# The opening of a two-block transformer kernel by feature blocks, with products on strips of TensorE's array

## The chip, the cores and the metric

The kernel runs on one core of a Trainium2 chip. Its engines work side by side and meet at semaphores: TensorE (matrix products; PE in the rows, PEld its weight loads), VectorE (DVE), ScalarE (ACT), GpSimd (POOL) and SyncE (SP), which here only issues loads. The metric is the device time of one execution in microseconds, lower is better. Three runs of the kernel before took 1216.97, 1219.66 and 1221.44 us.

## The reference

Two blocks of a network on 256 tokens of 1024 features, in float32. Only the start of the first block matters here:

```
mod(c)   = silu(c) @ w_ada + b_ada            # shift sh1, scale sc1, ...
h        = rmsnorm(x, g_mix) * (1 + sc1) + sh1
h_ctx    = rmsnorm(ctx, g_mix) * (1 + sc1c) + sh1c     # sh1c, sc1c from mod(c_ctx)
z        = h @ w_in  -> q, k, v, g, dd (32 columns), cb, cc, ch, ga, gb
zd       = dd @ w_dec_up + b_dec              # for two directions
log_a    = log_sigmoid(zd) / 16
o        = gated linear attention, forward and backward, over q, k, v, log_a,
           its start states from the same on ctx (k, v, log_a only)
```

Then come a convolution branch, gates, three feed-forward parts and a second block with two attentions.

## The kernel before

**Units.** The weights pass through the core in units of 256 columns (1 MB), loaded by SyncE into a ring of three buffers `raw`. ScalarE rounds a unit to `whi` (a short form of float32), VectorE takes the rest `wlo = raw - whi`, and TensorE makes three products for each: high by high, high by low, low by high. The activations are split in the same way: `A_hi`, `A_lo` for x and `B_hi`, `B_lo` for ctx. The order of the units of block one is the list `P1`: dd, two k, four v, two q, then the rest. The units dd, k and v are made for x and for ctx; a k or v unit has 96 products with a moving side of 256 columns. Every engine walks the same list in a loop over `u`, in which ScalarE first empties the PSUM banks of unit u - 1 (`evac1`), then rounds unit u + 2 (`split`), then does its part of the attention (`gla_front`, `gla_step`). The order on each engine is the order in which the code is written; nothing is reordered.

**The opening.** It must turn the two vectors c and c_ctx into shift and scale columns (one column for each block of 128 features), and x and ctx into the modulated, transposed, split activations. SyncE loads eight tiles `ada0[j]` of the modulation weights (1 MB each; tiles 0 to 3 give the shift, 4 to 7 the scale), the small vectors, ctx and x, then the units. TensorE multiplies the silu of c and c_ctx (two columns on the stationary side) by each tile (`L1272`, 2x256 outputs), turns the resulting row into columns (`L1756`), and transposes the normalized ctx and x (`norm`, `L1340`). ScalarE applies shift and scale to ctx (`modulate(0)`), VectorE to x (`affine`), both round and take rests. All 16 columns of all eight tiles are ready before the first feature is modulated. The dd unit follows with 48 products, then k0.

**The decays.** After the first half of k0 TensorE runs `decay_products` (passes 0 and 1; passes 2 and 3 follow within k1). A pass g is a direction and a pair of heads. ScalarE takes absolute values, exponentials and logarithms (`log_decays`, `soft_part`, `decays`), VectorE minima and running sums (`log_decays`, `sums`). These stand in the queues of both engines ahead of later splits and evacuations.

**GpSimd** computes 16 further modulation rows with its own multiply and add tree (`load_ada`, `adapt`, lines 748 and 756 to 759), one unit after the other, each load behind the end of the unit before. The first load waits for the opening's columns (`as_mm`), the first unit for the last rest of the activations (`hlo_done`, 16).

```
load_ada(0)
pool.wait_ge(hlo_done, 16)
for n in range(8):
    adapt(n)
    load_ada(n + 1)
```

Of the kernel before, what the change touches and what calls it, by code (L numbers as in the profile page):

```python
# [10 lines left out]
ALU = mybir.AluOpType  # L11
# [135 lines left out]
def build(nc, a, out):  # L147
    with ExitStack() as ctx:
# [72 lines left out]
        arow = ada_raw[0:2, :, :].rearrange("p a b -> p (a b)")  # L221

        ddT = arena[0:2 * RANK, 20 * KB:22 * KB].rearrange("p (s t) -> p s t", s=2)
# [21 lines left out]
        wdec = arena[0:2 * RANK, 77 * KB:81 * KB].rearrange("p (d n) -> p d n", d=2)  # L245
# [7 lines left out]

        XN = at3(24, TT, D)
        HF = at3(32, KD, T)
        HF1 = [at3(0, KD, T), at3(8, KD, T)]
# [63 lines left out]
        ada0_mm = sem("ada0_mm")  # L320
        ada0_row = sem("ada0_row")
# [145 lines left out]
        def unit_source(kind, n):  # L467
# [7 lines left out]
            if kind in first:  # L475
                w, c0 = first[kind]
                return cview(w, c0 + UC * n), KD, UC
# [20 lines left out]
        def _(sp):  # L498
            def load_unit(u, kind, n):
# [3 lines left out]
                dst = raw[ring(u)][:, 0:k * w].rearrange("p (k w) -> p k w", k=k)  # L503
# [49 lines left out]
            for j in range(8):  # L553
                if j == 2:

                    for name, r0 in VEC.items():
                        v = a[name]
                        n = math.prod(v.shape) // P
                        src = bass.AP(tensor=v.tensor, offset=0, ap=[[P, n], [1, P]])
                        sp.dma_start(vrows[r0:r0 + n, :], src).then_inc(vec_in, 16)  # L560
                    for name, r0, n in (("b_ada", 0, 48), ("b_ada_2", 48, 72)):
                        src = bass.AP(tensor=a[name].tensor, offset=0, ap=[[P, n], [1, P]])
                        sp.dma_start(brows[r0:r0 + n, :], src).then_inc(vec_in, 16)
                sp.dma_start(ada0[j], a["w_ada"][0].rearrange("(p k) n -> p k n", k=KD)[:, :, UC * j:UC * j + UC])\  # L564
                    .then_inc(start_ada[j], 16)
                if j == 3:
                    sp.dma_start(ctxX, a["ctx"].rearrange(tok, p=P)).then_inc(x_in[0], 16)
                    sp.dma_start(X[:], a["x"].rearrange(tok, p=P)).then_inc(x_in[1], 16)

            for u, (kind, n) in enumerate(P1):  # L570
                load_unit(u, kind, n)
# [37 lines left out]

        def norm_bank(n, b):  # L610

            return {0: (4, 5, 6, 0), 1: (1, 2, 3, 4), 2: (5, 6, 7, 2), 5: (4, 6, 7, 2)}.get(n, (4, 5, 6, 2))[b]
# [20 lines left out]

        def norm_fp32(n):
            return HF1[n] if n < 2 else HF

# [27 lines left out]
        def q_order(g):  # L664

            return 2 * (g % 2) + g // 2 + 1
# [1824 lines left out]
```

## Time and profile before

| | us |
|---|---|
| median of three runs | 1219.66 |
| profiled execution | 1218.4 |
| its span | 1216.6 |
| TensorE busy | 1166.5 (96%) |
| VectorE busy | 853.4 (70%) |
| ScalarE busy | 574.0 (47%) |
| GpSimd busy | 325.1 (27%) |

The busy rows of the page cut the span into 40 equal slices; a digit is the busy share in tenths, and PEclk the granted clock of TensorE in tenths of full speed. Rows of the timeline give the start, the time until the end of the last instruction merged into the row, and in brackets the idle time ahead and what ended it. A row that says x2 counts two instructions.

### The profile page before, as it was taken

The page shows a single profiled execution, that of the slowest core. Times are in us where ns is not written, and L with a number is a line of the kernel's source. Part 1 is how long each engine was busy: PE and PEld are TensorE (multiplying, and loading weights), DVE is VectorE, ACT ScalarE, POOL GpSimd, SP SyncE. Part 2 cuts the span into 40 slices and gives each one's busy share as a digit, 9 for nine tenths or more (in the row PEclk, how much of TensorE's full clock was granted, in tenths as well). Part 3 has the DMA queues.
Part 4 walks back from the last instruction along what each step waited for, and adds up shares of the span by engine and source line. Part 5 has one row for each costly group of instructions (what it writes and reads, how often), then busy time and mean ns, then how long its engine had stood idle before and what let it go on. Part 6 is the DMA issues. An engine that isn't in the chain of part 4 may idle for free.

```text
span 1216.6 us, 18692 instructions
## 1 busy us (share of the span) xinstructions
PE 1166.5 (96%) x7600; PEld 1040.7 (86%) x7600; DVE 853.4 (70%) x935; ACT 574.0 (47%) x734; POOL 325.1 (27%) x219
## 2 busy tenths in 40 slices
PE   6899999999999899999989999999999989999996
PEld 2599988999999888888878888889998989888885
DVE  0478474489577778877778877788766587755676
ACT  1566434354443364444555444445654625544452
POOL 1376573066565200000020000011156663000000
PEclk9899999999999899999989999999999989999999
DMA  9643645365866648777747777755954655656670
GB/s 310 218 139 105 208 144 168 105 217 186 273 232 218 203 169 275 242 254 257 267 147 255 254 252 246 261 161 190 298 181 149 201 186 179 204 177 201 213 258 35
DMA packets 192354, 250.59 MB, mean 206 GB/s; under 512 B 4763, under 2 KB 171870, under 8 KB 192158
## 3 DMA queue, kind: packets, MB, share of 16 engines
q1 hardware_dynamic: 183838, 217.44, 54.9%
q0 software_dynamic: 8448, 32.18, 7.7%
q8 instruction: 50, 0.82, 0.3%
q14 instruction: 18, 0.15, 0.0%
HBM read 248.56 MB, written 1.05 MB: 205 GB/s over the span
## 4 chain that ended last, share of the span: by engine, by line
PE 77%; DVE 13%; ACT 4%; issue 3%; SPq 2%; DMA 1%; POOL 0%; POOLq 0%; DVEq 0%; ACTq 0%
PE twin L1272 74%; DVE arena L1819 4%; DVE wlo L1819 3%; ACT arena L838 2%; DVE arena L1827 2%; SPq L564 1%; DMA raw<-in_w_in 1%; ACT whi L838 1%; PE twin L1340 1%; DVE X L1819 1%; DVE A_both L1819 1%; PE twin L1607 0%; DVE B_lo L1819 0%; DVE X L1827 0%; ACT L838 0%
## 5 line engine op out<-in xcount | busy, mean ns | idle before, releaser
L1272 PE MATMUL twin<-A_both,whi 128*128 128x256 f32 (+1 forms) x2224 | 584.7, 340 | 2.5 <-DVE arena L1819 1.1
L1819 DVE TENSOR_TENSOR wlo<-raw,whi 128x2048 fp32r<-128x2048 f32 x170 | 422.0, 2484 | 158.9 <-ACT whi L838 158.8
L1272 PE MATMUL twin<-A_both,wlo 128*128 128x256 f32 x1640 | 440.1, 281 | 0.0
L838 ACT ACTIVATE whi<-raw 128x2048 fp32r<-128x2048 f32 x170 | 325.1, 1912 | 217.9 <-PE twin L1272 212.1
L1272 PEld LDWEIGHTS twin<-A_both,whi 128*128 128x128 f32 x2224 | 375.1, 191 | 45.9 <-issue 6.7
L1272 PEld LDWEIGHTS twin<-A_both,wlo 128*128 128x128 f32 x1640 | 312.3, 190 | 11.3 <-DVE A_both L1819 0.4
L838 ACT ACTIVATE arena<-twin 128x512 f32<-128x512 f32 (+6 forms) x168 | 88.8, 554 | 125.5 <-PE twin L1272 84.8
L838 ACT ACTIVATE arena<-arena 128x512 f32<-128x512 f32 (+7 forms) x132 | 70.0, 559 | 164.3 <-DVE arena L1819 128.6
L756 POOL TENSOR_TENSOR ada_raw<-ada_raw,arena 128x2048 f32<-128x2048 f32 x24 | 104.7, 4361 | 145.9 <-DMA ada_raw<-in_w_ada 135.0
L1272 PE MATMUL twin<-whi,A_both 128*128 128x256 f32 x640 | 123.9, 295 | 15.4 <-DVE A_both L1819 10.3
L1272 PE MATMUL twin<-whi,B_hi 128*128 128x512 f32 (+2 forms) x340 | 126.8, 373 | 0.2 <-DVE B_lo L1819 0.2
L1272 PE MATMUL twin<-arena 128*2 128x256 f32 (+11 forms) x752 | 115.8, 318 | 11.3 <-DMA arena<-in_w_ada 11.1
L1272 PE MATMUL twin<-wlo,B_hi 128*128 128x512 f32 (+2 forms) x340 | 125.2, 368 | 0.0
L1272 PE MATMUL twin<-whi,B_lo 128*128 128x512 f32 (+2 forms) x340 | 125.2, 368 | 0.0
L1272 PEld LDWEIGHTS twin<-whi,A_both 128*128 128x128 f32 x640 | 105.2, 202 | 17.2 <-DVE A_both L1819 10.7
L1272 PEld LDWEIGHTS twin<-arena 128*128 128x128 f32 (+6 forms) x752 | 79.6, 155 | 39.4 <-issue 15.6
L1819 DVE TENSOR_TENSOR arena<-arena,twin 128x512 f32<-128x512 f32 x92 | 62.3, 684 | 62.4 <-ACT arena L838 49.3
L720 POOL TENSOR_SCALAR arena<-arena 128x1 f32<-128x1 f32 x4 | 1.6, 393 | 375.4 <-ACT arena L838 375.3
L1827 DVE SCALAR_TENSOR_TENSOR arena<-ada_raw,arena 128x256 f32 (+1 forms) x196 | 95.1, 485 | 7.0
L1272 PE MATMUL twin<-wlo,A_both 128*128 128x256 f32 x320 | 93.4, 292 | 0.0
L1272 PEld LDWEIGHTS twin<-whi,B_lo 128*128 128x128 f32 x340 | 64.2, 189 | 11.3 <-issue 0.7
L1272 PEld LDWEIGHTS twin<-wlo,B_hi 128*128 128x128 f32 x340 | 64.2, 189 | 10.7
(128 smaller groups left out, 1203.7 us busy)
## 6 DMA issues: line engine op xcount, KB each, us to landing
raw<-in_w_in SPq DMA_DIRECT2D x49, 1024.0 KB, 5.8
raw<-in_ffn_w_in SPq DMA_DIRECT2D x44, 1024.0 KB, 5.1
ada_raw<-in_w_ada POOLq DMA_DIRECT2D x28, 1024.0 KB, 6.2
ada_raw<-in_w_ada SPq DMA_DIRECT2D x24, 1024.0 KB, 5.4
raw<-in_w_ffn_in SPq DMA_DIRECT2D x22, 1024.0 KB, 5.1
raw<-in_ffn_w_out SPq DMA_DIRECT2D x22, 1024.0 KB, 5.0
raw<-in_w_ffn_out SPq DMA_DIRECT2D x11, 1024.0 KB, 5.1
arena<-in_w_ada SPq DMA_DIRECT2D x8, 1024.0 KB, 11.9
```

The costliest lines, as they stand in the source:

```text
L564: sp.dma_start(ada0[j], a["w_ada"][0].rearrange("(p k) n -> p k n", k=KD)[:, :, UC * j:UC * j + UC])\
L720: link(nc.gpsimd.tensor_scalar(p[0], p[0], EPS, None, ALU.add))
L756: link(nc.gpsimd.tensor_tensor(v[:], v[:], c3[:, :, s:s + 1].to_broadcast([P, KD, UC]), ALU.mult))
L838: return nc.scalar.activation(o, i, f, **kw)
L1272: return nc.tensor.matmul(o, l, r, start=start, stop=stop, **kw)
L1340: ins = nc.tensor.transpose(bank[norm_bank(n, b)][:, c:c + P], src[:, t, P * k:P * k + P], ident)
L1819: return nc.vector.tensor_tensor(o, x, y, op)
L1827: return nc.vector.scalar_tensor_tensor(out=o, in0=x, scalar=sc, in1=y, op0=op0, op1=op1)
```

## The change

The opening is done in four quarters of two feature blocks (256 features) each. A quarter q needs only the tiles q (shift) and 4 + q (scale). The modulation product now has 32 stationary columns (c, c_ctx and 30 of zeros) and is made in four strips of 32 array columns: shift and scale, two blocks each, land on four groups of 32 partitions of bank 3. One copy, one 128x128 transpose and three column operations give the quarter's shift and scale. dd is no longer a unit of the ring: its weights (128 columns loaded) stay in float32 and are multiplied, unsplit, with the float32 activations, again in four strips (x and ctx, two halves of the tokens). The key unit k0 is made in four parts, one behind each quarter. The decay products use four groups of 32 rows of the array, one for each strip of dd, and write to four banks; they come after the whole of k0, and their weights are loaded four times. The transposes of the decayed keys move half a unit and a unit later. GpSimd's first modulation load waits for the last columns and for dd, since its buffer now holds the dd weights and the rows of the opening.

```diff
@@ banks and buffers @@
-            b = [0, 7] if kind == "dd" else [0]
+            b = [0]
+        dd_out = at(20, P)
+        ada_flat = ada_raw[:, :, :].rearrange("p k n -> p (k n)")
+        c_wide = ada_flat[:, 0:KD * 32].rearrange("p (k s) -> p k s", k=KD)
+        start_rows = [ada_flat[:, 256 + P * q:384 + P * q] for q in range(4)]
+        dd_w = ada_flat[:, 768:768 + KD * P].rearrange("p (k w) -> p k w", k=KD)
...
+        start_h = [[at(8 * q + 2 * s, 512).rearrange("p (k t) -> p k t", k=2) for q in range(4)] for s in range(2)]
@@ SyncE's loads @@
+            load_start(0)
+            load_start(4)
+            sp.dma_start(ctxX, a["ctx"].rearrange(tok, p=P)).then_inc(x_in[0], 16)
...
+            sp.dma_start(X[:], a["x"].rearrange(tok, p=P)).then_inc(x_in[1], 16)
+            load_unit(0, *P1[0])
+            load_unit(1, *P1[1])
+            for j in (1, 5, 2, 6, 3, 7):
+                load_start(j)
@@ GpSimd @@
-                    pool.wait_ge(as_mm, 1)
+                    pool.wait_ge(start_cols, 4)
+                    pool.wait_ge(unit_used, 1)
...
-            for d in range(2):
-                pool.dma_start(wdec[RANK * d:RANK * d + RANK, d, :], a["w_dec_up"][0, d]).then_inc(dec_in, 16)
+            for i in range(4):
+                for d in range(2):
+                    r0 = 2 * RANK * i + RANK * d
+                    pool.dma_start(wdec[r0:r0 + RANK, d, :], a["w_dec_up"][0, d]).then_inc(dec_in, 16)
+            norm(0)
+            norm(1)
@@ ScalarE @@
+            def start_quarter(q):
+                h, ks = start_h[1][q], slice(2 * q, 2 * q + 2)
+                act.wait_ge(start_mod, q + 1)
+                act.wait_ge(tr_done, start_turned(0, q))
+                for m in range(2):
+                    k = 2 * q + m
+                    ins = run(h[:, m, :], bank[norm_bank(0, q)][:, T * m:T * m + T], ACT.Identity,
+                              bias=shift[:, 1, k:k + 1], scale=scale[:, 1, k:k + 1])
+                ins.then_inc(h_done, 1)
+                act.wait_ge(h_done, q + 1)
+                run(B_hi[:, ks, :], h).then_inc(hhi_done, 1)
+                act.wait_ge(h_dve, q + 1)
+                run(A_hi[:, ks, :], start_h[0][q]).then_inc(hhi_done, 1)
@@ TensorE @@
-            def decay_products(g):
-
-                d, p, order = gla_pass(g)
-                if g == 0:
-                    pe.wait_ge(dec_in, 32)
+            def decay_products(g0):
+                if g0 == 0:
+                    pe.wait_ge(dec_in, 128)
                     pe.wait_ge(consts, 1)
                     pe.wait_ge(act_evac, EV1[0][1])
-                if g >= 2:
-                    pe.wait_ge(z_min, 2 * (g - 2) + 2)
-                for s in range(2):
+                else:
+                    pe.wait_ge(z_min, 2 * g0)
+                for g in (g0, g0 + 1):
+                    d, p, order = gla_pass(g)
                     for h in range(2):
-                        c = HK * (2 * p + h)
-                        ins = mm(bank[2 * (g % 2) + s][:, T * h:T * h + T], wdec[:, d, c:c + HK], ddT[:, 1 - s, :],
-                                 True, True)
-                    ins.then_inc(zd_mm, 1)
+                        for i in range(4):
+                            r, c = slice(32 * i, 32 * i + 32), HK * (2 * p + h)
+                            o = T * (g % 2) + P * h
+                            ins = mm(bank[i][:, o:o + P], wdec[r, d, c:c + HK], dd_out[r, :], True, True)
+                ins.then_inc(zd_mm, 4)
...
-                if (u, half) == (U_V + 2, 0):
+                if (u, half) == (U_V + 3, 0):
                     pe.wait_ge(ek_done, 4)
...
-                if (u, half) == (U_V + 3, 0):
+                if (u, half) == (U_V + 3, 1):
...
+            def start_modulation(q):
+                if q:
+                    pe.wait_ge(start_mod, q)
+                pe.wait_ge(start_ada[q], 16)
+                pe.wait_ge(start_ada[4 + q], 16)
+                for k in range(KD):
+                    for i in range(4):
+                        x, m = divmod(i, 2)
+                        ins = mm(bank[3][32 * i:32 * i + 32, 0:P], c_wide[:, k, :],
+                                 ada0[4 * x + q][:, k, P * m:P * m + P], k == 0, k == KD - 1)
+                ins.then_inc(start_mm, 1)
+            def turn_rows(q):
+                pe.wait_ge(start_row, q + 1)
+                nc.tensor.transpose(bank[3][:, T:T + P], start_rows[q], ident).then_inc(start_cols, 1)
+            def decay_quarter(q):
+                if q == 0:
+                    pe.wait_ge(landed[0], 16)
+                    pe.wait_ge(vec_done, 1)
+                pe.wait_ge(h_done, q + 1)
+                pe.wait_ge(h_dve, q + 1)
+                for m in range(2):
+                    k = 2 * q + m
+                    for i in range(4):
+                        x, th = 1 - i // 2, i % 2
+                        ins = mm(bank[0][32 * i:32 * i + 32, 0:P], dd_w[:, k, 0:2 * RANK],
+                                 start_h[x][q][:, m, P * th:P * th + P], k == 0, k == KD - 1)
+                if q == 3:
+                    ins.then_inc(unit_used, 1)
+            def key_part(q):
+                if q == 0:
+                    pe.wait_ge(lo_ready, 2)
+                    pe.wait_ge(vec_done, 1)
+                b = BANKS1[1]
+                for x, o in ((B, bank[b[1]]), (A, bank[b[0]])):
+                    pe.wait_ge(hlo_done, 4 * q + (2 if x is B else 4))
+                    for half in range(2):
+                        for k in (2 * q, 2 * q + 1):
+                            ins = step_product(1, o[:, T * half:T * half + T], x, half, False, k,
+                                               k == 0 and half == 0, None, False)
+                if q == 3:
+                    ins.then_inc(unit_used, 1)
...
+            start_modulation(0)
+            pe.wait_ge(ident_done, 1)
+            pe.wait_ge(vec_in, 16 * (len(VEC) + 2))
+            nc.tensor.transpose(bank[6][:, 0:NVEC], vrows[0:NVEC, :], ident[0:NVEC, 0:NVEC])
+            nc.tensor.transpose(bank[6][:, P:P + BROWS], brows[0:BROWS, :], ident[0:BROWS, 0:BROWS])\
+                .then_inc(vec_tr, 1)
+            turn_rows(0)
+            start_turn(0, 0, 1)
+            start_turn(1, 0, 1)
+            start_modulation(1)
+            decay_quarter(0)
+            turn_rows(1)
+            key_part(0)
+            start_turn(0, 2)
+            start_turn(1, 2)
+            start_modulation(2)
+            decay_quarter(1)
+            turn_rows(2)
+            key_part(1)
+            start_turn(0, 3)
+            start_turn(1, 3)
+            start_modulation(3)
+            decay_quarter(2)
+            turn_rows(3)
+            key_part(2)
+            decay_quarter(3)
+            key_part(3)
+            gla(U_K, 0)
@@ VectorE @@
+            def start_quarter(q):
+                ks = slice(2 * q, 2 * q + 2)
+                start_columns(q)
+                dve.wait_ge(start_mod, q + 1)
+                dve.wait_ge(tr_done, start_turned(1, q))
+                for m in range(2):
+                    k = 2 * q + m
+                    ins = ts(start_h[0][q][:, m, :], bank[norm_bank(1, q)][:, T * m:T * m + T],
+                             scale[:, 0, k:k + 1], shift[:, 0, k:k + 1], ALU.mult, ALU.add)
+                ins.then_inc(h_dve, 1)
+                for s, (hi, lo) in ((1, (B_hi, B_lo)), (0, (A_hi, A_lo))):
+                    dve.wait_ge(hhi_done, 2 * q + (1 if s else 2))
+                    rest(lo[:, ks, :], start_h[s][q], hi[:, ks, :]).then_inc(hlo_done, 2)
```

The order that this gives, first on TensorE. Before, from the last shift tile to the first transposes of ctx:

```order
L1272 MATMUL twin<-arena 2x256 [waits start_ada3]
L1272 MATMUL twin<-arena 2x256 x7
L1742 MATMUL twin<-arena 128x75 [waits vec_in,ident_done]
L1743 MATMUL twin<-arena 128x120
L1272 MATMUL twin<-arena 2x256 [waits start_ada4]
L1272 MATMUL twin<-arena 2x256 x7
L1272 MATMUL twin<-arena 2x256 [waits start_ada5]
L1272 MATMUL twin<-arena 2x256 x7
L1340 MATMUL twin<-arena 128x128 [waits xn_done]
L1340 MATMUL twin<-arena 128x128 x3
L1340 MATMUL twin<-arena 128x128 [waits vec_done]
L1340 MATMUL twin<-arena 128x128
```
After, the last quarter; the rows left out are key products (24 to a part):

```order
L1286 MATMUL twin<-arena,ada_raw 32x128 [waits start_ada7,start_ada3,start_mod]
L1286 MATMUL twin<-arena,ada_raw 32x128 x31
L1286 MATMUL twin<-arena,ada_raw 32x128 [waits h_dve,h_done]
L1286 MATMUL twin<-arena,ada_raw 32x128 x7
L1758 MATMUL twin<-arena,ada_raw 128x128 [waits start_row]
L1286 MATMUL twin<-B_hi,whi 128x256 [waits hlo_done]
...
L1286 MATMUL twin<-A_both,whi 128x256 [waits hlo_done]
...
L1286 MATMUL twin<-arena,ada_raw 32x128 [waits h_dve,h_done]
L1286 MATMUL twin<-arena,ada_raw 32x128 x7
L1286 MATMUL twin<-B_hi,whi 128x256 [waits hlo_done]
```
The tiles are waited for in pairs, and the last pair has one key part of the quarter before, a dd quarter, and its own dd and key part behind it.

SyncE's queue, before, from the last small vector to the units:

```order
L563 DMA arena<-in_b_ada 72x128
L564 DMA arena<-in_w_ada 128x8x256 x2
L567 DMA arena<-in_ctx 128x2x1024
L568 DMA X<-in_x 128x2x1024
L564 DMA arena<-in_w_ada 128x8x256 x4
L504 DMA raw<-in_w_in 128x8x256 x3
```
After, from the first tiles; the small vectors are left out:

```order
L562 DMA arena<-in_w_ada 128x8x256 x2
L567 DMA arena<-in_ctx 128x2x1024
...
L575 DMA arena<-in_b_ada 72x128
L576 DMA X<-in_x 128x2x1024
L512 DMA ada_raw<-in_w_in 128x8x128
L512 DMA raw<-in_w_in 128x8x256
L562 DMA arena<-in_w_ada 128x8x256 x6
L512 DMA raw<-in_w_in 128x8x256
```
The dd weights and k0 now stand ahead of six of the modulation tiles, and ctx ahead of the small vectors.

## Rows read from the trace of the kernel before

**Rows 1.** Timeline, TensorE: start us, us, engine line op, out<-in, count, [idle <-releaser]
```profile
36.50 1.97 PE L1340 MATMUL twin<-arena 128*128 128x128 f32 x16
...
61.96 0.51 PE L1272 MATMUL twin<-A_both,whi 128*128 128x256 f32 x2 [0.87 <-DVE wlo L1819]
...
67.90 3.72 PE L1272 MATMUL twin<-arena 32*128 32x256 f32 x16
...
122.03 0.47 PE L1272 MATMUL twin<-whi,A_both 128*128 128x256 f32 x2 [3.10 <-ACT arena L838]
```

**Rows 2.** Timeline, ScalarE, 41 to 121 us
```profile
41.40 1.91 ACT L838 ACTIVATE whi<-raw 128x2048 fp32r<-128x2048 f32 x1 [4.20 <-DMA raw<-in_w_in]
...
69.07 3.43 ACT L838 ACTIVATE arena<-twin,arena 128x256 f32<-128x256 f32 x8 [5.50 <-PE twin L1272]
...
120.82 1.06 ACT L838 ACTIVATE arena<-twin 128x512 f32<-128x512 f32 x2
```

**Rows 3.** Timeline, VectorE, the running sums of the four passes
```profile
78.07 0.69 DVE L1819 TENSOR_TENSOR arena<-arena 128x512 f32<-128x512 f32 x1 [4.67 <-ACT arena L838]
...
78.80 1.27 DVE L2044 TENSOR_TENSOR_SCAN arena<-arena 128x256 f32<-128x256 f32 x2
...
81.95 3.93 DVE L1819 TENSOR_TENSOR arena<-arena 128x512 f32<-128x512 f32 x1
...
85.91 2.20 DVE L2063 COPY arena<-arena 128x2 f32<-128x2 f32 x1
...
88.82 2.74 DVE L2044 TENSOR_TENSOR_SCAN arena<-arena 128x256 f32<-128x256 f32 x2
...
94.16 0.17 DVE L2063 COPY arena<-arena 128x2 f32<-128x2 f32 x1
...
104.00 2.75 DVE L2047 TENSOR_TENSOR_SCAN arena<-arena 128x256 f32<-128x256 f32 x2
...
113.37 3.93 DVE L1819 TENSOR_TENSOR arena<-arena 128x512 f32<-128x512 f32 x1
...
117.33 2.24 DVE L2063 COPY arena<-arena 128x2 f32<-128x2 f32 x1
```

**Rows 4.** Stretches: us, busy (instructions) of each engine, granted clock, DMA share, GB/s
```profile
33.00:36.00 3.00, 3.00 (x16) 1.17 (x15) 0.81 (x1) 0.00 (x0) 2.86 (x7) 1.00 1.10 351
...
122.00:172.00 50.00, 49.97 (x366) 48.25 (x367) 26.45 (x30) 19.67 (x26) 29.89 (x14) 0.97 0.59 190
...
370.00:401.00 31.00, 24.82 (x193) 23.66 (x192) 24.12 (x16) 9.74 (x8) 22.13 (x9) 0.93 0.60 200
```

**Rows 5.** Chain that ended last: start us, us, what
```profile
31.09 13.66 DMA raw<-in_w_in
...
131.25 11.51 PE twin L1272 x96
```

**Rows 6.** Timeline, TensorE: full products at low clock, then products on strips
```profile
52.26 0.41 PE L1272 MATMUL twin<-B_hi,wlo 128*128 128x256 f32 x1
...
52.47 0.41 PE L1272 MATMUL twin<-B_hi,whi 128*128 128x256 f32 x1
...
180.92 1.25 PE L1272 MATMUL twin<-arena 128*32 128x64 f32 x64 [0.19 <-DVE arena L1819]
...
191.27 0.28 PE L1272 MATMUL twin<-A_both,wlo 128*128 128x256 f32 x1
...
191.48 1.95 PE L1272 MATMUL twin<-arena 128*64 128x256 f32 x16
```

**Rows 7.** Timeline, GpSimd: its modulation units
```profile
47.92 0.96 POOL L748 DMA_DIRECT2D ada_raw<-in_w_ada  x1 [9.36 <-PE twin L1756]
...
59.79 9.99 POOL L756 TENSOR_TENSOR ada_raw<-ada_raw,arena 128x2048 f32<-128x2048 f32 x1 [10.91 <-DVE A_both L1819]
...
80.91 4.42 POOL L756 TENSOR_TENSOR ada_raw<-ada_raw,arena 128x2048 f32<-128x2048 f32 x1 [5.28 <-DMA ada_raw<-in_w_ada]
...
244.10 0.30 POOL L683 TENSOR_SCALAR arena<-arena 128x4 f32<-128x4 f32 x1 [45.74 <-ACT arena L838]
```

More of the change, by code:

```diff
@@ L476, in unit_source @@
                 w, c0 = first[kind]
-                return cview(w, c0 + UC * n), KD, UC
+                width = P if kind == "dd" else UC
+                return cview(w, c0 + UC * n, width), KD, width
             if kind == "uq":
@@ L838, in run, with split @@
                 return nc.scalar.activation(o, i, f, **kw)
[L840 removed]
+            def split(u, i=0, count=1):
                 if isinstance(i, int) and u + 3 * i >= UNITS:
@@ L846, in split @@
                     act.wait_ge(unit_used, lin(3, i, u - RING + 1))
-                run(whi[ring(u)][:], raw[ring(u)][:]).then_inc(hi_ready, 1)
+                run(whi[ring(u)][:], raw[ring(u)][:]).then_inc(hi_ready, count)
             def squares(n):
@@ L1222, in _ @@
             squares(0)
-            act.wait_ge(ada0_mm, 1)
-            run(arow[:, 0:512], bank[0][0:2, :]).then_inc(ada0_row, 1)
             squares(1)
-            for b in range(1, 4):
-                if b == 3:
-                    split(0)
-                    split(1)
-                act.wait_ge(ada0_mm, b + 1)
-                run(arow[:, 512 * b:512 * b + 512], bank[b][0:2, :]).then_inc(ada0_row, 1)
-            modulate(0)
-            modulate(1)
+            start_quarter(0)
+            split(1, count=2)
+            start_quarter(1)
+            start_quarter(2)
+            start_quarter(3)
+            split(2)
             for u in range(N1):
@@ L1302, in first_product @@
             def first_product(u, o, x, halves, token_major, low, before, w0=None):
-                each = 1 if low is hlo_done and before >= low_count(2) else 2
+                each = 1 if low is hlo_done else 2
                 for b in range(KD // each):
-                    pe.wait_ge(low, before + (2 * b + 2 if low is hlo_done and each == 2 else b + 1))
+                    pe.wait_ge(low, before + b + 1)
                     for half in range(halves):
@@ L1837, in split @@
                 dve.wait_ge(hi_ready, lin(3, i, u + 1))
-                rest(wlo[ring(u)][:], raw[ring(u)][:], whi[ring(u)][:]).then_inc(lo_ready, 1)
+                rest(wlo[ring(u)][:], raw[ring(u)][:], whi[ring(u)][:]).then_inc(lo_ready, count)
             def adapt(n, i, dst, blk):
@@ L2399, in second @@
                 evac2(N2 - 1)
+            start_copy(0)
             norm(0)
             norm(1)
-            split(0)
-            dve.wait_ge(vec_done, 1)
-            columns(0, 7, VEC["g_mix"], 0, (0, 1))
-            for b in range(4):
-                low(0, b)
-                dve.wait_ge(tr_done, 4 + b + 1)
-                for k in (2 * b, 2 * b + 1):
-                    ins = affine(1, k)
-                ins.then_inc(h_dve, 1)
-            for b in range(4):
-                low(1, b)
-            split(1)
+            start_quarter(0)
+            split(1, count=2)
+            start_quarter(1)
+            start_quarter(2)
+            start_quarter(3)
+            split(2)
             for u in range(N1):
```

242 lines of the change are left out of this document (105 added, 137 removed).

## Prediction

> **What bounds the kernel now.** I began with the page's engine shares. TensorE is busy for 96% of the span, so the opening, where it is not, is the only stretch in which much can be won. The timeline of TensorE shows the first product of the first key unit k0 at 61.96 and the decay products, 16 instructions, at 67.90; the third value unit, v2, starts at 122.03 after a wait of 3.10 us [rows 1].
>
> The chain of waits says why v2 is late, and it is not TensorE. From 67.90 on it runs over ScalarE (the eight absolute values, 3.43 us from 69.07, then exponentials and logarithms) and VectorE (the running sums of the four passes, from 78.07), and comes back to TensorE only when ScalarE has emptied the banks of v0, at 120.82 for 1.06 us, behind the last exponentials of the fourth pass [rows 2, 3]. So between the start of the decay products, which I call D, and the start of v2 lie 122.03 - 67.90 = 54.1 us, whatever TensorE does. After v2 the table by stretches shows TensorE busy for 49.97 of 50 us [rows 4]. What brings v2 forward is therefore kept, up to later waits such as the 6.2 us that TensorE loses between 370 and 401 (24.82 busy of 31). The question is when D comes, and how long the 54.1 us are afterwards.
>
> **Term 1, the last modulation weights.** The eight weight tiles of the modulation are now waited for in pairs (0 and 4, 1 and 5, and so on), and the last pair is queued behind 11.5 loads of 1 MB in all (two tiles, ctx, x, half a load for dd, k0, six tiles). In the old queue the eleventh load landed at 41.40, when ScalarE began on it after a wait for it [rows 2], and the twelfth at 31.09 + 13.66 = 44.75 [rows 5]. 11.5 loads give 43.1. The transfers run at 351 GB/s [rows 4], 3.0 us a load; the dd load has rows half as wide, so it may cost a whole load (+1.5), and GpSimd's small decay weights now go four times and early (at most +0.7, their 0.19 MB at that rate). I take 44.3, between 43 and 46.
>
> **Term 2, from there to D.** TensorE has then in its queue, in this order: modulation quarter 3 (32 products, 64 instructions of 128 columns), a dd quarter (16 instructions), one transpose, the key part of quarter 2 (24 products), a dd quarter and the last key part (24).
> The key parts have the shape of all unit products: 96 take 11.51 us [rows 5], 0.12 us each, so 2.9 us a part; at the lower clock the spacing is 52.47 - 52.26 = 0.21, so 5.1 [rows 6].
> The products on a strip of the array have no row of quite this shape. Decay products cost 3.72 / 16 = 0.232 us for an instruction of 256 columns [rows 1], so 0.116 for 128 one after the other: 64 of them 7.4 us. With two strips of 64 columns, 16 instructions of 256 columns took 1.95 us, 0.122 each instead of 0.232, so they ran beside each other. With four strips, 64 instructions of 32 and 64 columns took 1.25 us, 0.020 each [rows 6], which is an issue limit. Four strips of 128 columns should then need 7.4 / 4 = 1.9 us, with bounds 1.3 and 7.4. I take 2.2, the nearest row being the 0.122, twice as good again with twice the strips, and 0.5 for a dd quarter.
> Sum at full clock: 2.2 + 0.5 + 0.4 + 2.9 + 0.5 + 2.9 = 9.4 us. The VectorE and ScalarE work of quarter 3 (a copy, column operations, two affines, two roundings, two rests) is some seven steps on a path, each near the 0.69 us of a 512-wide VectorE operation at 78.07 [rows 3], so about 5 us; it lies beside the transpose and the key part of quarter 2. I add 1.7 us for a stretch at low clock, what v2 loses now after its wait. D = 44.3 + 9.4 + 1.7 = 55.4, against 67.90: 12.5 us earlier. With all at low clock it is up to 15.6 us from the landing, without loss 8.8.
>
> The two places of the skill that bear on this. The rows show 1.9 times the rate for two strips. The Trainium skill ("TensorE: Matmul & The Clock Gate", Part 3) has 2.38 times for three strips of columns measured; scaled to four, about 3.1, an estimate of that page, the modulation quarter would take 2.4 us where I have 2.2.
> Going from full products to strips costs little in the rows: the last full product at 191.27 is followed by the first strip product at 191.48, 0.21 instead of 0.12 [rows 6]. The Trainium skill ("TensorEngine Tiling (Array Packing)", Key Properties) speaks against the change: it says that another tiling mode first drains the engine. With the row's 0.09 us, six such changes behind the landing are 0.5 us, inside the 1.7 above.
>
> **Is TensorE ready for the last quarter?** Pair 1 and 5 is behind 7.5 loads, so it lands at about 41.40 - 3.5 x 3.05 = 30.7. A quarter of work between two modulations is 2.2 + 0.5 + 0.3 + 2.9 and eight transposes (16 took 1.97 us [rows 1]), 1.0: 6.9 us, against 6.1 for two loads. Quarter 3 can start at 30.7 + 2 x 6.9 = 44.5: the landing and TensorE end together. The 64 old modulation products and the 48 of dd are gone with the time they took before 61.96; no work that remains was hidden by them.
>
> **Term 3, from D to v2.** The decay products become 32 row-strip instructions per two passes instead of 16, of half the columns: no row shows strips of rows in four banks, so they cost between 3.72 / 4 = 0.9 and 3.7 us. ScalarE now waits for all of them, where it began 1.17 us after the first. That is between -0.2 and +2.6; I take +0.5, as for columns.
> The other part is GpSimd. Rows of VectorE in the sums last longer whenever GpSimd's modulation units run: 3.93 us for an operation that takes 0.69 at 78.07, 2.20 for a copy that takes 0.17 at 94.16, scan pairs of 2.74 and 2.75 against 1.27, then 3.93 and 2.24 again [rows 3]. The first ends at 85.88, just after GpSimd's product of 80.91 + 4.42 [rows 7]. Excess: 3.2 + 2.0 + 1.5 + 1.5 + 3.2 + 2.1 = 13.5 us, nearly all on the chain.
> Now the first unit is loaded at 47.92 and starts at 59.79, 8 us before D; the next starts at D + 13.0 [rows 7]. Afterwards its load waits for the last dd quarter, about D - 3, and comes 6.2 us later (0.96 to issue and 5.28 of waiting for the second unit), so it runs from about D + 3.5 to D + 12, before the sums, which begin at D + 10.2. The second unit falls to D + 18.5: the first two passes meet it only at their end, and the last two meet the third unit nearly whole. I count 6.8 us for a unit in the sums, the first three of the list, and 1 to 3 for the grazing one, so about 9.5 instead of 13.5: -4, between -8 and +3.
> Sum: 54.1 + 0.5 - 4.0 = 50.6 us. v2 starts at 55.4 + 50.6 = 106.0, 16.0 us earlier. TensorE has until then k1, v0, v1 and the decays, about 38 us from D, and so waits some 12 us instead of 3; that is covered by the chain, and I add 1 us for a longer stretch at low clock behind it. The key transposes go one half unit later; they wait less there and cost the same.
>
> **Sum.** 1218.4 (the profiled run, whose span is 1216.6) - 16.0 + 1.0 = 1203.4. The median of the runs is 1.3 us above that run, so 1204.7: I say 1205 us. Ends: 43 + 8.8 + 45.9 = 97.7 for v2 is 24 us gained (1195); 46 + 15.6 + 59.7 = 121.3 is 1 us gained (1219).
>
> **Rivals.**
> A, no relief: the GpSimd units meet the sums as before, or one more does. Speaking for it, each load waits for the end of the unit before, and its time hangs on VectorE's. Gain 12.5 + 0 - 1 - 0.5 = 11 us: 1209; with 3 us more stall 1212.
> B, half at low clock: between the quarters TensorE waits for weights, and low clock shows in the trace where it had worked with gaps (0.21 at 52.3). Quarters of 9 to 10 us put the last one at 50 and D near 62: 1213.
> C, slower: the quarters, not the loads, set the pace, since the strips run one after the other or the clock stays low. In a row, a modulation quarter is 7.4 and a dd quarter 1.9, a quarter of work 13.5 us; the last starts at 57.7 and D is 57.7 + 7.4 + 1.9 + 0.4 + 2.9 + 1.9 + 2.9 = 75.1, v2 at 127.6: 1225. At low clock throughout (4.4 + 1.0 + 0.5 + 5.1 + 2.0 = 13.0 a quarter) D is 73.8 and v2 124.4: 1222. It decides from about 12 to 13 us a quarter. Against it stand the 0.020 and 0.122 us of the strip rows and that a queue so full keeps TensorE busy.
> D, given back: the later wait of 6.2 us doubles as GpSimd shifts against the units. Gain 16 less 1 and 6: 1211. Beyond the opening nothing else is short: GpSimd stands idle for 45.74 us before the head norms [rows 7].
>
> **Chances.** Forecast 0.55, A 0.17, B 0.10, D 0.07, C 0.08, something else 0.03. About 0.5% (6 us, 1213.6 and 1225.8) can be told from no change. The forecast, A and D lie nearly whole below 1213.6, B half. Faster 0.81, same 0.11, slower 0.08 (most of C and the rest). Range 1196 to 1216: the forecast with its bounds, A, D and most of B.
>
> **What would show it.** The 64-instruction modulation groups should last near 2.2 us; the last pair should land at 43 to 46; D at 53 to 60; v2 at 50 to 52 us behind D with at most two long VectorE rows of 3.9; TensorE's wait for v2 near 12 us. The forecast is wrong if a modulation quarter takes over 7 us, if D is beyond 65, or if v2 comes forward and the end does not.

## The result and the profile after

The changed kernel took 1208.86 us (median of four runs, 1204.21 to 1210.98), the kernel before, on the same chip, 1220.55: a ratio of 0.990 [0.987, 0.993], 11.7 us less. The prediction was 1205 us, faster with 0.81. The profiled executions took 1210.52 and 1218.4 us, with spans of 1208.5 and 1216.6, so between these two only 8.1 us lie.

The page of the kernel after, its span and busy time of the engines:

```profile
span 1208.5 us, 19055 instructions
PE 1135.7 (94%) x7764; PEld 1027.4 (85%) x7764; DVE 861.6 (71%) x944; ACT 569.5 (47%) x729; POOL 325.1 (27%) x226
```

TensorE is busy for 30.8 us less, yet idle for 72.8 us instead of 50.1. The gain is what is left of 30.8 after 22.7 us of new waiting.

Timeline of TensorE after; these rows answer to [rows 1]:

```profile
31.40 4.49 PE L1286 MATMUL twin<-arena,ada_raw 128*32 128x128 f32 x80 [3.97 <-DMA arena<-in_w_ada]
...
38.73 0.28 PE L1286 MATMUL twin<-A_both,wlo 128*128 128x256 f32 x1
38.85 0.60 PE L1771 MATMUL twin<-arena 128*128 128x128 f32 x4
...
39.82 2.39 PE L1286 MATMUL twin<-arena,ada_raw 128*32 128x128 f32 x80
...
46.19 2.39 PE L1286 MATMUL twin<-arena,ada_raw 128*32 128x128 f32 x80
...
51.47 0.28 PE L1286 MATMUL twin<-A_both,wlo 128*128 128x256 f32 x1
51.67 0.64 PE L1286 MATMUL twin<-arena,ada_raw 128*32 128x128 f32 x16
...
55.31 1.17 PE L1286 MATMUL twin<-arena 32*128 32x128 f32 x32
...
93.40 0.77 PE L1286 MATMUL twin<-whi,A_both 128*128 128x256 f32 x2 [12.43 <-ACT arena L864]
...
109.62 0.47 PE L1286 MATMUL twin<-whi,A_both 128*128 128x256 f32 x2 [2.80 <-ACT arena L864]
```

A group x80 is a modulation quarter (64) with the dd quarter of the quarter before behind it (16). Quarter 1 waits 3.97 us for its weights and takes 4.49 us where the later groups take 2.39; the granted clock is 0.50 there, the lower of its two levels, as the window shows (its last three numbers are the granted clock, the DMA share and GB/s):

```profile
32.00:34.00 2.00, 2.00 (x48) 2.00 (x43) 1.02 (x1) 0.00 (x0) 0.00 (x0) 0.50 1.10 347
```

Quarters 2 and 3 wait for nothing and follow each other in 46.19 - 39.82 = 6.4 us. The decay products, 32 now, start at 55.31 (D), 12.6 us earlier than in [rows 1]. The value unit v1 waits 12.43 us for ScalarE, v2 another 2.80, and v2 starts at 109.62: 12.4 us earlier, with 54.3 us between D and it, against 54.1.

Timeline of VectorE after, the running sums, to be laid beside [rows 3]:

```profile
58.15 3.23 DVE L1897 TENSOR_SCALAR arena<-twin,arena 128x256 f32<-128x256 f32 x8 [0.23 <-ACT arena L864]
65.16 1.56 DVE L1892 TENSOR_TENSOR arena<-arena 128x512 f32<-128x512 f32 x1 [3.78 <-ACT arena L864]
66.75 2.75 DVE L2145 TENSOR_TENSOR_SCAN arena<-arena 128x256 f32<-128x256 f32 x2
...
72.98 1.27 DVE L2145 TENSOR_TENSOR_SCAN arena<-arena 128x256 f32<-128x256 f32 x2
...
76.13 3.93 DVE L1892 TENSOR_TENSOR arena<-arena 128x512 f32<-128x512 f32 x1
80.09 2.21 DVE L2164 COPY arena<-arena 128x2 f32<-128x2 f32 x1
...
94.71 3.92 DVE L1892 TENSOR_TENSOR arena<-arena 128x512 f32<-128x512 f32 x1
98.67 2.25 DVE L2164 COPY arena<-arena 128x2 f32<-128x2 f32 x1
...
101.63 2.76 DVE L2148 TENSOR_TENSOR_SCAN arena<-arena 128x256 f32<-128x256 f32 x2
```

Timeline of GpSimd after, beside [rows 7]:

```profile
60.07 3.61 POOL L779 TENSOR_TENSOR ada_raw<-ada_raw,arena 128x2048 f32<-128x2048 f32 x1 [6.13 <-DMA ada_raw<-in_w_ada]
...
69.25 0.95 POOL L771 DMA_DIRECT2D ada_raw<-in_w_ada  x1 [0.30 <-POOL arena L782]
75.25 4.26 POOL L779 TENSOR_TENSOR ada_raw<-ada_raw,arena 128x2048 f32<-128x2048 f32 x1 [5.04 <-DMA ada_raw<-in_w_ada]
79.59 2.69 POOL L780 TENSOR_TENSOR ada_raw<-ada_raw 128x1024 f32<-128x1024 f32 x1
...
93.53 4.56 POOL L779 TENSOR_TENSOR ada_raw<-ada_raw,arena 128x2048 f32<-128x2048 f32 x1 [5.80 <-DMA ada_raw<-in_w_ada]
98.16 2.73 POOL L780 TENSOR_TENSOR ada_raw<-ada_raw 128x1024 f32<-128x1024 f32 x1
```

The pairs belong together: the VectorE row of 76.13 ends at 80.06, GpSimd's product at 79.51; the 128x2 copy ends at 82.30, GpSimd's sum at 82.28. Against the undisturbed lengths in [rows 3] the seven long rows are 14.4 us too long. Before it was 13.9 us, the 13.5 of the prediction and 0.4 of an operation at 102.87 that took 1.09 us instead of 0.69. The whole stall of the sums is still there, under other units. It is GpSimd's arithmetic that does it and not its loads: the load issued at 69.25 was under way until 75.2 (GpSimd waits for it for 5.04 us), and the scans at 72.98 have their short length.

After v2 part of the gain is lost at the first state products. VectorE and TensorE of the kernel after:

```profile
154.47 6.88 DVE L1892 TENSOR_TENSOR arena<-arena 128x512 f32<-128x512 f32 x2
```
```profile
162.10 3.75 PE L1286 MATMUL twin<-arena 64*128 64x256 f32 x8 [2.80 <-DVE arena L1892]
```

The same two VectorE instructions took 1.29 us at 165.95 before. GpSimd had a product there (153.96 for 4.08 us, then 2.69). TensorE waits 2.80 us and then works at a granted clock of 0.51 from 162 to 168; the lead over the kernel before falls from 11.5 us at 154 to 5.5 at 170. It comes back in part and is 8.1 at the end.

### The profile page after: what moved, and what is told of

It is laid out like the page before. It is cut to its first block, busy times and chain, and to the rows that moved or that the text cites. A ratio compares the mean times of both kernels' runs of the same rounds, so it can differ in the third digit from the quotient of the medians.

```text
span 1208.5 us, 19055 instructions
## 1 busy us (share of the span) xinstructions
PE 1135.7 (94%) x7764; PEld 1027.4 (85%) x7764; DVE 861.6 (71%) x944; ACT 569.5 (47%) x729; POOL 325.1 (27%) x226
## 3 DMA queue, kind: packets, MB, share of 16 engines
HBM read 248.23 MB, written 1.05 MB: 206 GB/s over the span
## 4 chain that ended last, share of the span: by engine, by line
PE 75%; DVE 14%; ACT 4%; issue 4%; SPq 2%; DMA 1%; POOL 0%; POOLq 0%; DVEq 0%; ACTq 0%
PE twin L1286 73%; DVE arena L1892 5%; DVE wlo L1892 4%; ACT arena L864 2%; DVE arena L1900 2%; ACT whi L864 1%; DVE X L1892 1%; DMA arena<-in_w_ada 1%; PE twin L1347 1%; DVE arena L2175 1%; SPq L512 1%; PE twin L1612 0%; DVE X L1900 0%; SPq L562 0%; DVE arena L1896 0%
## 5 line engine op out<-in xcount | busy, mean ns | idle before, releaser
L1286 PEld LDWEIGHTS twin<-A_both,whi 128*128 128x128 f32 x2208 | 371.3, 190 | 44.7 <-issue 6.9
L864 ACT ACTIVATE arena<-twin 128x512 f32<-128x512 f32 (+5 forms) x167 | 88.4, 555 | 116.6 <-PE twin L1286 85.7
L779 POOL TENSOR_TENSOR ada_raw<-ada_raw,arena 128x2048 f32<-128x2048 f32 x24 | 98.1, 4089 | 136.7 <-DMA ada_raw<-in_w_ada 136.7
L1286 PEld LDWEIGHTS twin<-whi,A_both 128*128 128x128 f32 x640 | 105.4, 202 | 29.7 <-issue 16.2
L1286 PE MATMUL twin<-arena 128*128 128x1 f32 (+10 forms) x656 | 80.3, 296 | 2.8 <-DVE arena L1892 2.8
L780 POOL TENSOR_TENSOR ada_raw<-ada_raw 128x1024 f32<-128x1024 f32 x24 | 76.1, 3169 | 1.9
L1286 PEld LDWEIGHTS twin<-arena 128*128 128x128 f32 (+5 forms) x656 | 65.5, 171 | 10.7 <-issue 3.0
```

The costliest lines, as they stand in the source:

```text
L779: link(nc.gpsimd.tensor_tensor(v[:], v[:], c3[:, :, s:s + 1].to_broadcast([P, KD, UC]), ALU.mult))
L780: link(nc.gpsimd.tensor_tensor(v[:, 0:4, :], v[:, 0:4, :], v[:, 4:8, :], ALU.add))
L864: return nc.scalar.activation(o, i, f, **kw)
L1286: return nc.tensor.matmul(o, l, r, start=start, stop=stop, **kw)
```

## The experiments

Each is the changed kernel with the edit named, run beside the kernel before. Beside the plain hold, the six and ten, the strips in turn and the old place of the transposes that took a median of 1223.28 us, beside the other four 1219.41.

**GpSimd held back until the sums are done.**

```diff
             pool.wait_ge(hlo_done, 16)
+            pool.wait_ge(d_done, 4)
             for n in range(8):
```

> The changed kernel, but GpSimd's first modulation unit also waits until the running sums of all four passes are done. Theory (GpSimd's units stretch the sums): the long VectorE rows (3.93, 2.21, 3.92, 2.25 and scan pairs of 2.75 us) become 0.7, 0.2 and 1.3; that is 14.4 us of the 54.3 us from the decay products (D) to v2. D stays at 55.3, the chain shrinks to about 40, v1 starts near 86 and v2 near 98, now bound by TensorE's own products. Eight units of 17.4 us from about 95 then end near 235, some 5 us after the head norms would need GpSimd, so part is given back: 1200 to 1205 us, from 1209. Rival (the long rows have another cause, such as weight loads landing in the same memory): v2 stays at 109 to 110 and the end is later than the changed kernel's, 1209 to 1215.

Measured: 1199.91 us, ratio 0.981 [0.978, 0.983], span 1199.8. TensorE, ScalarE and VectorE do the same work as after. Timelines of GpSimd, VectorE and TensorE in this kernel:

```profile
91.78 5.54 POOL L779 TENSOR_TENSOR ada_raw<-ada_raw,arena 128x2048 f32<-128x2048 f32 x1 [39.01 <-DVE arena L1893]
```
```profile
63.98 0.69 DVE L1893 TENSOR_TENSOR arena<-arena 128x512 f32<-128x512 f32 x1 [3.78 <-ACT arena L865]
64.71 1.28 DVE L2146 TENSOR_TENSOR_SCAN arena<-arena 128x256 f32<-128x256 f32 x2
...
90.67 0.69 DVE L1893 TENSOR_TENSOR arena<-arena 128x512 f32<-128x512 f32 x1
...
93.75 4.11 DVE L1893 TENSOR_TENSOR arena<-arena 128x510 f32<-128x510 f32 x1
```
```profile
54.13 1.17 PE L1287 MATMUL twin<-arena 32*128 32x128 f32 x32
...
84.61 0.77 PE L1287 MATMUL twin<-whi,A_both 128*128 128x256 f32 x2 [4.81 <-ACT arena L865]
...
98.06 0.40 PE L1287 MATMUL twin<-whi,A_both 128*128 128x256 f32 x2
```

Every row of the sums has its short length. The operation of 128x510 at 93.75, which comes after the sums and during GpSimd's first product, takes 4.11 us; in the kernel after it took 0.68, at 109.35, where GpSimd had no product. v1 comes 8.8 us earlier than after, and v2 at 98.06 without a wait: 43.9 us behind D instead of 54.3. So 10.4 us of the way to v2 were GpSimd's doing. The rest of the 14.4 us of stall is hidden here, since TensorE works without a pause from v1 on; in the experiment with the earlier evacuation below, v2 starts 40.7 us behind D, 13.6 less than 54.3. The cost appears later, since the eighth unit ends at 225.5: TensorE waits 1.05 us at 232.16 and 1.89 at 245.80, which it doesn't do in the kernel after.

**The hold, with six units ahead of the roots and ten behind** (the same edit, and `range(8)` made `range(6)` in the first loop, the second loop from 6).

> As e1_hold, and only six of GpSimd's modulation units stand ahead of its work for the head norms, ten behind it, instead of eight and eight. Theory: v2 near 98 as there, and nothing is waited for at the head norms (six units end near 200, the norms come near 228). The sixteenth unit ends some 20 us later relative to TensorE, which has room before the feed-forward part. 1195 to 1200 us. Rival: the late last units are waited for, or the clashes with VectorE only move to the conv and head-norm stretch: 1203 to 1209.

Measured: 1208.4 us, 0.989 [0.986, 0.992]: no better than after. The profiled run is one of two near 1216 (span 1214.4), the other four took 1205.88 to 1208.79, so the trace shows the loss larger than the median has it. The roots come at 219.37 and the two waits are gone, as expected, but the chunk of ten ends at 416.6, and the norm of the next part stands behind it in GpSimd's queue. Timeline of TensorE:

```profile
418.72 3.68 PE L1348 MATMUL twin<-arena 128*128 128x128 f32 x16 [23.87 <-DVE arena L1897]
```

The theory of the expectation missed this, and its rival (the late last units are waited for, 1203 to 1209) named it. The queue of GpSimd had not been read to its end.

**The hold, with seven and nine.**

> As e1_hold (GpSimd's first unit behind the running sums), with seven units ahead of the head norms and nine behind. With eight, the eighth unit ended at 225.5 and the roots for the head norms came at 226.8 us, where with six they came at 219.4; with six, the last unit ended at 416 and the norm before the feed-forward part, queued behind it on GpSimd, made TensorE wait 23.9 us. Theory (the queue of GpSimd decides on both sides): with seven the roots come near 219.5 and the last unit ends at 392 to 398, just before the norm's partial sums at 398: 2 to 6 us less than e1_hold, 1194 to 1198. Rival: VectorE's head norms are late for other reasons, or the last unit is late again: 1199 to 1206.

Measured: 1195.28 us (1193.83 to 1197.33), 0.979 [0.976, 0.982], span 1195.3, the lowest median of all. TensorE's timeline:

```profile
55.70 1.17 PE L1287 MATMUL twin<-arena 32*128 32x128 f32 x32
...
86.19 0.77 PE L1287 MATMUL twin<-whi,A_both 128*128 128x256 f32 x2 [4.82 <-ACT arena L865]
...
258.64 0.77 PE L1287 MATMUL twin<-whi,A_both 128*128 128x256 f32 x2 [2.31 <-DVE arena L1893]
```

D is 1.6 us later than with the plain hold, and still the end is 4.5 us earlier; from 225 to 258 TensorE has no wait of 0.25 us or more. GpSimd's norm of the next part comes at 395.92, early enough. By the ratios alone seven and nine can't be told from eight and eight, since the intervals overlap (0.981 [0.978, 0.983] for the plain hold). But the hold with the earlier evacuation, measured beside it, has the waits of the plain hold at 232.44 and 246.08 and took 1198.57 to 1201.33 us in its five runs, all above the highest of these.

**The strips in turn.** The modulation and dd products in another order, each strip of the array with all its contractions before the next strip:

```diff
-                for k in range(KD):
-                    for i in range(4):
+                for i in range(4):
+                    for k in range(KD):
```

> The changed kernel with the products of the modulation and of dd in another order: all products of one strip of 32 columns one after the other, then the next strip, instead of the four strips in turn. The same products, the same results. Theory (the four strips run beside each other only when neighbours in the queue are on different strips): 64 instructions go from 2.0 us to about 7.4 (0.116 each, half of the 0.232 of 256 columns), a dd quarter from 0.4 to 1.9, D from 55.3 to 70 to 76, the end 15 to 20 us later: 1223 to 1229. Rival (the 0.030 us an instruction is what any 32-wide product takes, whatever its neighbour): nothing moves, 1209.

Measured: 1220.55 us, 0.999 [0.997, 1.002]. TensorE's timeline:

```profile
42.88 6.39 PE L1286 MATMUL twin<-arena,ada_raw 128*32 128x128 f32 x80
...
62.70 0.66 PE L1286 MATMUL twin<-arena,ada_raw 128*32 128x128 f32 x16
...
66.35 1.17 PE L1286 MATMUL twin<-arena 32*128 32x128 f32 x32
```

The same view of the window from 43.00 to 44.20 us, inside the first strip:

```profile
42.88 1.50 PE L1286 MATMUL twin<-arena,ada_raw 128*32 128x128 f32 x12
```

A group of 80 instructions takes 6.39 us against 2.39, with the same operands. Its mean of 0.080 us hides two costs. Within one strip the instructions follow each other at 0.11 us: the twelve of the window end after 1.50 us, and one of them alone lasts 0.27, so eleven steps take 1.23. That is about the 0.116 that the prediction worked out. But the 16 instructions of a dd quarter, which are now four to a strip before the next strip, take 0.66 us, as they did in the other order (0.64). Short runs on a strip still overlap with the next strip, runs of 16 hardly. Taken together this gives a smaller loss than expected: D is at 66.35, not at 70 to 76, but 11.0 us later than after, and the whole gain is gone. Four strips side by side are what the change lives from. This is rival C's mechanism, milder because the strips overlap at their ends.

**The key parts all behind the last quarter** (`key_part(0)` to `(2)` moved behind `decay_quarter(3)`).

> The changed kernel with the four key parts all behind the last dd quarter, as one block, instead of one part behind each quarter. Theory (the parts fill TensorE between the modulations, whose pace was 6.37 us a quarter, and the weights' landing is not the bound): without them a quarter costs TensorE 3.5 us less, the modulation of quarter 3 waits for its weights and starts at 43 to 45 instead of 46.2, which shows when the last pair lands; D = 44 + 2.4 + 4.5 (columns, affines, dd) + 11.6 = 61 to 64 instead of 55.3. End 6 to 8 us later, 1215 to 1217, if the shift is kept. Rival (the opening is bound by the landing, the parts are hidden either way): D moves by under 3 us, 1209 to 1211.

Measured: 1218.38 us, 0.997 [0.995, 0.999]. Timelines of TensorE and VectorE:

```profile
43.03 2.39 PE L1286 MATMUL twin<-arena,ada_raw 128*32 128x128 f32 x80 [2.29 <-DMA arena<-in_w_ada]
...
61.26 1.17 PE L1286 MATMUL twin<-arena 32*128 32x128 f32 x32
...
119.49 0.47 PE L1286 MATMUL twin<-whi,A_both 128*128 128x256 f32 x2 [2.89 <-ACT arena L864]
```
```profile
103.29 4.63 DVE L2158 TENSOR_TENSOR_SCAN arena<-arena 128x512 f32<-128x512 f32 x1
```

Now TensorE is ahead of the loads, and the trace shows when they land: the last pair at 43.0. In the changed kernel TensorE reaches it at 46.19, so its own work, not the load, sets D there. Of the 12.6 us of D, 6.0 are owed to the key work that lies between the quarters. The end is later than the 1215 to 1217 expected, and GpSimd is why: v2 comes 58.2 us behind D instead of 54.3. GpSimd's units fall on other rows of the sums here, the scan at 103.29 for instance takes 4.63 us instead of 1.23, and all long rows together are 18.3 us too long instead of 14.4. The 3.9 us of more stall are the 3.9 us of longer chain. So the meetings price the chain in this kernel too, where nothing was held.

**The key transposes at their old places** (the waits and `ctx_key_tokens` half a unit and a unit earlier).

> The changed kernel with the transposes of the decayed keys, and ScalarE's copies of them, at their old places (behind the first halves of v2 and of v3). Theory: TensorE reaches them at about 116 and waits for the last decayed key, which is ready at 121.3: a wait of 5 us and a stretch at low clock behind it, while v3 would have waited until 123.5 in any case; v3 starts near 130 instead of 123.5. Of this some 6 us stay: 1213 to 1216. Rival (the move is worth nothing, since v3 waits for its weights' rest anyway): 1208 to 1210.

Measured: 1216.34 us, 0.996 [0.993, 0.999]. TensorE's timeline:

```profile
121.47 3.47 PE L1400 MATMUL twin<-arena 128*128 128x128 f32 x16 [6.17 <-DVE arena L1892]
```

TensorE waits 6.17 us that the changed kernel doesn't. The prediction had priced the move at nothing (and as half a unit, which is right for one of the two groups; the other moved a whole unit). The comparison says 0.6% of the whole (0.996 beside 0.990 and 0.990), with intervals that just overlap. In the first trace of the changed kernel the loss can't be seen at the start after the first attention (276.72 there, 276.98 here), because that execution lost 6.0 us at 162 to GpSimd. The second trace of the changed kernel, which comes last below, was spared this, and against it the loss is plain:

```profile
276.98 0.47 PE L1286 MATMUL twin<-whi,A_both 128*128 128x256 f32 x2 [2.89 <-DVE arena L1892]
```

There this start is at 271.21, 5.8 us earlier, and the first state product at 154.34 against 159.42. At the end 4.8 us are left (spans 1213.8 and 1209.0), near the 6 us expected.

**Evacuation of k1 earlier, with the hold** (`evac1(U_K + 1)`, the second key unit, moved ahead of `soft_part(2)` on ScalarE).

> As e1_hold, and ScalarE empties the banks of the second key unit behind the absolute values of passes 2 and 3, ahead of their exponentials and logarithms, instead of one unit of its loop later. In e1_hold the start of v1 waits 4.81 us for that evacuation. Theory (behind the hold the evacuation order is the next bound, TensorE itself would be free): v1 starts 4 to 5 us earlier without a wait, v2 only as early as ScalarE's chain allows, about 95 to 96 instead of 97.5; 1 to 4 us off the end: 1196 to 1199. Rival: the 1.06 us evacuation now stands in the chain of the sums and v2 gets nothing: 1200.

Measured: 1199.7 us, 0.983 [0.980, 0.985]: the same as the hold alone. TensorE's timeline:

```profile
95.26 0.47 PE L1289 MATMUL twin<-whi,A_both 128*128 128x256 f32 x2 [3.55 <-ACT arena L865]
...
109.67 0.50 PE L1289 MATMUL twin<-whi,A_both 128*128 128x256 f32 x2 [1.17 <-DVE wlo L1895]
```

The wait of v1 goes, and one of 3.55 us at v2 and one of 1.17 at v3 come. v2 starts 2.8 us earlier than with the hold alone (95.26 against 98.06), but the granted clock is 0.64 from 95 to 99, and v3 starts at 109.67 against 109.58. The wait only moves along.

**The changed kernel once more.**

> The changed kernel once more, unaltered, beside the next ones, for the size of its scatter. 1204 to 1211 us. If the stretch from v2 to the head norms differs between this profile and the first (where the start of v2 was 12.4 us earlier than in the kernel before, and 5.5 us were left behind the head norms), the loss there is a matter of chance meetings of GpSimd and VectorE; if it is the same, it is fixed by the order.

Measured: 1211.14 us (five runs at 1210.55 to 1211.47, one at 1200.36), 0.990 [0.987, 0.994]. Timelines of VectorE and TensorE:

```profile
154.57 1.29 DVE L1892 TENSOR_TENSOR arena<-arena 128x512 f32<-128x512 f32 x2
```
```profile
271.21 0.77 PE L1286 MATMUL twin<-whi,A_both 128*128 128x256 f32 x2 [2.89 <-DVE arena L1892]
...
391.35 0.79 PE L1286 MATMUL twin<-whi,A_both 128*128 128x256 f32 x2 [4.24 <-DVE A_both L1892]
```

The clash of GpSimd and VectorE behind 154 isn't there, and at 271.21 this execution is 11.0 us ahead of the kernel before (282.22). But it ends with the same span, 1209.0. The windows behind that wait, of this run and then of the kernel before:

```profile
273.00:275.00 2.00, 2.00 (x12) 2.00 (x11) 2.00 (x3) 0.56 (x1) 0.00 (x0) 0.50 0.79 281
275.00:277.00 2.00, 2.00 (x11) 2.00 (x11) 1.97 (x3) 0.00 (x0) 1.20 (x1) 0.50 0.98 314
```
```profile
284.00:286.00 2.00, 2.00 (x19) 2.00 (x18) 2.00 (x3) 0.57 (x1) 0.00 (x0) 1.00 0.62 234
```

Before, TensorE waited 2.09 us there and its granted clock stayed 1.00, the higher level. Now it waits 2.89, and the clock is 0.50 until about 277: the same 921 instructions up to the wait near 391 keep it busy for 114.9 us instead of 111.7. So 3.2 us are given back by low clock behind a wait that became 0.8 us longer. Shown is the clock and the sum, not that the longer wait is its cause.

## Why the prediction was right, point by point

The time lay in the stated range and the kernel became faster, as forecast. One term of the sum, the relief from GpSimd, brought nothing, and the range held the result because it had allowed for that. D came out right in part by coincidence.

**Term 1** (last pair at 44.3, between 43 and 46): the load lands at 43.0 in the experiment in which TensorE waits for it; in the trace after, the last issue is 0.7 us later (31.5 against 30.8), so it lands near 43.7, an estimate. It did not bind; TensorE's pace of 6.4 us a quarter did. The prediction had called this a tie (quarter 3 at 44.5), and the group starts at 46.19.

**Term 2** (9.4 + 1.7 us, D = 55.4): D came at 55.31. Four strips cost 0.030 us an instruction, so 1.9 us for the 64, where I took 2.2; a key part cost 2.9. The granted clock is 1.00 from 36 to 56, so the 1.7 us for low clock were not spent behind the landing: from 46.19 to D are 9.1 us where I had 11.1. They were spent two quarters earlier. The group at 31.40 took 2.1 us more than the later ones, at a granted clock of 0.50, and that is most of why quarter 3 began 1.9 us later than the 44.3 I had assumed. So D is right to 0.1 us by two errors of about 2 us in opposite directions, and the 0.1 us is chance also in another way: in seven traces with this opening D lies between 54.13 and 55.70. One bound was summed wrongly: with all at low clock the prediction's own terms give 4.4 + 1.0 + 0.4 + 5.1 + 1.0 + 5.1 = 17.0 us from the landing, as its rival C has it, and not 15.6. Nothing came near it. That 0.020 us an instruction is an issue limit, no run shows.

**Term 3, the products** (+0.5): ScalarE's absolute values ended 4.6 us behind D before (69.07 + 3.43) and 4.3 after (56.55 + 3.03). Right, slightly better. Rival C's serial strips didn't come.

**Term 3, relief from GpSimd** (-4.0): this is the term that was mis-sized; the mechanism was right. The stall was to fall from 13.5 to about 9.5 us and measured 14.4. With the products, 0.3 us shorter, the whole chain from D to v2 changed by +0.2 us instead of -3.5. I had the first unit run from D + 3.5 to D + 12, the second from D + 18.5, and allowed 1 to 3 us for the one that only grazes the sums. In the trace the first runs from D + 4.8 to D + 13.7 and stretches two rows (2.4 us), and the second, at D + 19.9, stretches two more (5.3 us). It hits an instruction of the second pass whole, and then the copy. The third runs from D + 38.2 and costs 6.8 us, as I had counted. Two units met the first passes, not one, and a unit that meets a single VectorE instruction costs its full product and the sum behind it. The hold shows what the term could have brought: 10.4 us. So rival A's mechanism, which had 0.17, is what happened, and its time of 1209 us is that of the median. Part of that agreement is luck: rival A counted 1 us lost behind v2, and the profiled pair lost about 4.

**What TensorE does meanwhile** (waits some 12 us instead of 3): it waited 12.43 and 2.80. Right.

**After v2** (kept, but for 1 us): too little. By the profiled executions 12.4 us at v2 became 8.1 at the end. In one execution 6.0 us went at 162, in the other that was spared and 3.2 went to low clock behind 271. Rival D (given back at the wait of 6.18 us in the kernel before) didn't come: that wait is 4.23 and 4.24.

**Rival B** didn't come: the quarters took 6.4 us. Only the group of quarter 1 ran at low clock.

**The sum**: 16.0 - 1.0 = 15 us were forecast. Of D's 12.5 all came, of the relief's 3.5 nothing, and of what lies behind v2 about 4 more were lost in the profiled pair. The medians show 11.7 us [9.2, 16.2]. The time lay in the range since its ends took in a stall of the old size. The medians differ by 3.6 us more than the profiled pair, and that the time came within 4 us of 1205 is owed to this too.

**The two rules of the Trainium skill.** The Trainium skill ("TensorE: Matmul & The Clock Gate", Part 3) led to an estimate of 3.1 times for four strips. The traces give 0.11 / 0.030 = 3.7, with the step within one strip from the strips in turn. The Trainium skill ("TensorEngine Tiling (Array Packing)", Key Properties) names a drain at a new tiling mode. The trace agrees, and it is small: the first strip product of the dd quarter starts at 51.67, 0.20 us behind the last full product at 51.47, where 0.12 is usual, and the transposes at 38.85, which use the full array, follow the full product at 38.73 by 0.12.

**Left open.** Why one of six runs took 1200.36 us. Whether the clash at 162 falls away in such runs can't be told, since neither of the two traced executions is one of them; the second trace was spared the clash and took 1211.01 us all the same.

## What to carry to other kernels

Products on separate strips of the array pay if the queue changes strips often. Here runs of four instructions on one strip cost nothing, and runs of 16 lost most of the gain. When a stretch is moved forward, what runs beside it is not moved with it: list which units of the other engine fall on the moved chain, instruction by instruction, and price each meeting at the full length of the other engine's operation. One wait that keeps GpSimd out of a chain on VectorE took the ratio here from 0.990 to 0.981, nearly as much again as the rewriting of the opening gave. A held engine has to be read to the end of its queue, for the next part's norm stood behind it.

## What the runs showed of the hardware

A VectorE instruction of the sums that starts while a GpSimd operation runs is held until about the end of that operation, however small it is: a copy of 128x2 took 2.21 us instead of 0.17, and an operation of 128x512 3.93 instead of 0.69. The Trainium skill ("SBUF — State Buffer", SBUF: two separate sides) says that the two share a pair of ports which the one that starts first holds for its whole instruction; the paired ends above agree. It doesn't hold for every instruction: the eight minima at 58.15, whose input is TensorE's output (`twin`), took 3.23 us beside GpSimd's product of 60.07, and 3.23 us in the hold, where GpSimd stood idle.

TensorE instructions of 128 columns on one strip of the array follow each other at 0.11 us; with four strips side by side one costs 0.030 us.

TensorE's granted clock stayed at 1.00 behind a wait of 2.09 us and was 0.50 for some 6 us behind one of 2.89. Behind the 2.50 us at 276.72 of the first trace it was 1.00 until 278, 0.53 until 280 and 0.61 until 282, and behind the 12.43 us at 93.40 it was 0.50 and back by about 97. So neither did the longest wait cost more, nor does the length of the wait alone tell when the clock falls.
